# Weight sums of the first up-projection block by accumulating DMA, shorter row sums on GpSimd, earlier loads for the second block

## What is computed

```python
mix = jnp.einsum('btm,md->btd', jnp.concatenate([attn, c], axis=-1), w_out) + b_out
x = layer_norm(ALPHA * x + mix, ln1_g, ln1_b)
h = jnp.einsum('btd,df->btf', x, ffn_w_up)          # 2048 -> 2 x 5504
h, new_ffn = causal_dwconv(ffn_hist, h, ffn_conv_w, ffn_conv_b)   # 3 taps
hu, hg = jnp.split(h, 2, axis=-1)
f = jnp.einsum('btf,fd->btd', jax.nn.silu(hg) * hu, ffn_w_down)
x = layer_norm(ALPHA * x + f, ln2_g, ln2_b)
```

## Time and profile before

| | us |
|---|---|
| median of three runs | 2166.41 (2166.27 to 2168.33) |
| the profiled execution | 2166.84 |
| its span, first to last instruction | 2165.1 |
| TensorE busy (matmuls) | 2073.1, 96% of the span |
| VectorE busy | 1417.8, 65% |
| ScalarE busy | 910.3, 42% |
| GpSimd busy | 421.8, 19% |

### The profile page before, as it was taken

The page is one execution under the profiler, slowest core; times in us unless marked ns, Lnnn a source line. Parts: engine busy times, 40 slices in busy tenths (PEclk is TensorE's granted clock), DMA queues, the critical chain, the costliest instruction groups (busy, mean ns, idle before and its releaser), DMA issues.

```text
span 2165.1 us, 41651 instructions
## 1 busy us (share of the span) xinstructions
PE 2073.1 (96%) x16109; PEld 2045.3 (94%) x16117; DVE 1417.8 (65%) x1918; ACT 910.3 (42%) x1264; POOL 421.8 (19%) x543
## 2 busy tenths in 40 slices
PE   8999999799984999999999999999999999999995
PEld 8999999699984999999999999999999999999994
DVE  3788888677587877777877777777764222334324
ACT  4344444333464555554455555454443111222223
POOL 0113122020630221121212121212121000004222
PEclk9999999799996999999999999999999999999998
DMA  6322222023545666666767676767658222332222
GB/s 223 103 77 74 73 75 85 20 69 113 175 141 185 184 190 179 186 182 183 189 184 185 181 186 179 199 174 191 178 180 291 91 89 88 118 108 86 86 78 83
DMA packets 93211, 306.36 MB, mean 142 GB/s; under 512 B 11908, under 2 KB 12676, under 8 KB 93120
## 3 DMA queue, kind: packets, MB, share of 16 engines
q1 hardware_dynamic: 74976, 243.22, 34.2%
q0 software_dynamic: 16992, 59.87, 14.3%
q10 hardware_dynamic: 1152, 1.96, 0.3%
HBM read 281.05 MB, written 23.97 MB: 141 GB/s over the span
## 4 chain that ended last, share of the span: by engine, by line
PE 86%; DVE 7%; issue 3%; ACT 2%; DMA 2%; POOL 0%; SPq 0%; ACTq 0%; POOLq 0%; DVEq 0%
PE acc L857 41%; PE acc L920 22%; PE acc L576 15%; PE acc L770 3%; PE acc L672 1%; PE acc L661 1%; PE acc L652 1%; DMA x_raw<-xT 1%; PE acc L585 1%; DVE resid L2031 0%; ACT w_hi L965 0%; DVE w_lo L1679 0%; DVE tb L1647 0%; DMA raw_a<-w_down 0%; DVE comb L1813 0%
## 5 line engine op out<-in xcount | busy, mean ns | idle before, releaser
L857 PE MATMUL acc<-comb,w_hi 128*128 128x274 f32 x4816 | 929.4, 292 | 29.3 <-DVE comb L1813 18.4
L857 PEld LDWEIGHTS acc<-comb,w_hi 128*128 128x128 f32 x4816 | 766.6, 190 | 30.9 <-issue 11.8
L857 PE MATMUL acc<-comb,w_lo 128*128 128x274 f32 x2408 | 698.6, 290 | 0.0
L920 PE MATMUL acc<-acts,w_hi 128*128 128x272 f32 x2752 | 461.4, 290 | 5.8 <-DVE resid L1975 2.2
L857 PEld LDWEIGHTS acc<-comb,w_lo 128*128 128x128 f32 x2408 | 462.2, 192 | 0.0
L920 PEld LDWEIGHTS acc<-acts,w_hi 128*128 128x128 f32 x2752 | 391.7, 189 | 6.8 <-issue 3.5
L920 PE MATMUL acc<-acts,w_lo 128*128 128x272 f32 x1376 | 285.5, 289 | 0.0
L1209 ACT ACTIVATE w_hi<-sum 128x1024 fp32r<-128x1024 f32 x172 | 182.2, 1059 | 231.2 <-PE acc L857 120.9
L1761 DVE TENSOR_TENSOR w_lo<-sum,w_hi 128x1024 fp32r<-128x1024 f32 x172 | 210.6, 1225 | 88.6 <-ACT w_hi L1209 85.5
L1761 DVE TENSOR_TENSOR w_lo<-raw_a,w_hi 128x1024 fp32r<-128x1024 f32 x127 | 155.0, 1221 | 98.9 <-ACT w_hi L1209 98.9
L920 PEld LDWEIGHTS acc<-acts,w_lo 128*128 128x128 f32 x1376 | 217.1, 189 | 0.0
(11 more groups left out here) (247 smaller groups left out, 2795.1 us busy)
## 6 DMA issues: line engine op xcount, KB each, us to landing
raw_a<-w_up SPq DMA_DIRECT2D x129, 512.0 KB, 6.2
stage<-w_stream SPq DMA_DIRECT2D x90, 512.0 KB, 3.5
sum<-w_up SPq DMA_DIRECT2D x87, 512.0 KB, 3.5
sum<-w_up POOLq DMA_DIRECT2D x86, 512.0 KB, 7.5
sum<-w_down SPq DMA_DIRECT2D x45, 448.0 KB, 3.3
sum<-w_down SPq DMA_DIRECT2D x24, 512.0 KB, 3.5
act_spill<-prod_f SPq DMA_DIRECT2D x43, 272.0 KB, 6.3
act_raw<-act_spill POOLq DMA_DIRECT2D x43, 272.0 KB, 4.1
```

The lines of the kernel that those rows point to most:

```text
L857: mm = pe.matmul(bank(BANK_OF[j]), wt[:, k * P:(k + 1) * P], prod_comb(j, k, b), start=start and q == 0, stop=stop and q == 2, skip_group_ ...
L920: mm = pe.matmul(acc[:, a, h, 0:D_TOK // 2], wt[:, w * P:(w + 1) * P], x[:, h * (D_TOK // 2):(h + 1) * (D_TOK // 2)], start=start and q == ...
```

## The change

1. Block 0's `sum_2` is made in DRAM-to-SBUF transfers: SyncE loads quarter 2 into it ahead of pass 20's weight, GpSimd adds quarter 3 after row sum 20 and quarter 0 after row sum 25, and, once VectorE has split it for product 1, quarter 1. `make_s2(0)` and `make_s4(0)` leave VectorE; blocks from 1 on keep both. `raw_a11` and `raw_a12` aren't loaded for block 0, and the counts of their semaphores are one lower from then on.
2. GpSimd sums `SUMMED` = 12 of the second half's rows. TensorE takes rows 12 to 15 itself: 12 and 13 in the middle of pass 31, 14 and 15 behind it. There are four buffers of squares instead of two.
3. Block 1's loads: A11 behind `sum_3` of block 0, `sum_1` and `sum_3` between and behind the last row stores, A12 and A22 behind them; GpSimd issues their accumulations ahead of its wait for the last split.

The diff, cut to its core (the three new semaphores' declaration is left out):

```diff
 ORDER0 = (1, 3, 4, 5, 2, 6, 7)
+SUMMED = KT - 4
 ROWS_AT = (0, 1, 3, 4, 5, 7, 8, 10)
...
-        resid = at("resid", [P, 2 * KT + 2, TOK], F32, r1)
+        resid = at("resid", [P, 2 * KT + 4, TOK], F32, r1)
         sq1 = resid[:, 2 * KT:, :]
...
-            square = 2 * KT + m % 2
+            square = 2 * KT + m % 4
             return resid[:, m:square + 1:square - m, half_cols[h]]
...
-            for i in range(N_OUT - 4):
-                if i == 2:
-                    sp.wait_ge(ln_out, CT)
-                load_out(i)
-
             def quarter(f, q):
...
-                sp.wait_ge(s2_made, f + 1)
+                sp.wait_ge(s2_made, f)
                 sp.wait_ge(up_lo, nth(f, 0))
...
                 sp.wait_ge(up_lo, nth(f, 4))
-                sp.wait_ge(s4_made, f + 1)
+                sp.wait_ge(s4_made, f)
                 load_a12(f + 1)
-                if p is not None:
-                    spill(f - 1, p)
+                spill(f - 1, p)
                 sp.wait_ge(up_lo, nth(f, 5))
...
-            load_a11(0)
-            load_s1(0)
-            for i in range(N_OUT - 4, N_PASS):
+            for i in range(N_PASS):
+                if i == 2:
+                    sp.wait_ge(ln_out, CT)
+                if i == KT + 4:
+                    sp.wait_ge(attn_out, KT)
+                    sp.dma_start(sum_2[:, :], dram["w_up"][2]).then_inc(s2_loaded, 16)
+                    load_s1(0)
                 load_out(i)
...
+            load_a11(1)
             for k in range(4):
...
             load_a22(0)
-            for k in range(4, 8):
+            for k in range(4, 6):
                 spill_rows(k, x1_spilled)
+            sp.wait_ge(up_lo, nth(0, 2))
+            load_s1(1)
+            for k in range(6, 8):
+                spill_rows(k, x1_spilled)
+            sp.wait_ge(up_lo, nth(0, 3))
+            load_s3(1)
             sp.wait_ge(x1_spilled, 64)
             sp.wait_ge(t_made, 16)
-            load_a12(0)
-            up_loads(0, None)
+            load_a12(1)
+            sp.wait_ge(up_lo, nth(0, 5))
+            load_a22(1)
             with sp.Fori(0, (FT - 4) // 3) as i:
...
             last = N_PROD * (FT - 1)
-            sp.wait_ge(s2_made, FT)
+            sp.wait_ge(s2_made, FT - 1)
             sp.wait_ge(up_lo, last + 1)
...
                         row_stats_begin()
+                        row_last(SUMMED)
+                        row_last(SUMMED + 1)
                     w = slice(k * P, (k + 1) * P)
...
-                pe.wait_ge(row_summed, KT + POOLED)
+                pe.wait_ge(row_summed, KT + SUMMED)
                 row_term(2, ln_sq1[:, 0, second_half], True, False)
                 row_term(3, ln_sq1[:, 1, second_half], True, False)
-                row_last(POOLED)
...
                 pe.wait_ge(row_squared, KT + m + 1)
-                return row_term(3, sq1[:, m % 2, second_half], False, m == KT - 1)
+                return row_term(3, sq1[:, m % 4, second_half], False, m == KT - 1)
...
                     row_term(1, ln_sq1[:, 1, first_half], True, True).then_inc(row_stat, 1)
+            row_last(KT - 2)
             row_last(KT - 1).then_inc(row_stat, 1)
...
                 act.wait_ge(row_added, i + 1)
-                if i >= 2:
-                    act.wait_ge(row_summed, i - 1)
-                act.activation(sq1[:, m % 2, t], resid[:, m, t], ACT.Square).then_inc(row_squared, 1)
+                if i >= 4:
+                    act.wait_ge(row_summed, i - 3)
+                act.activation(sq1[:, m % 4, t], resid[:, m, t], ACT.Square).then_inc(row_squared, 1)
...
             def hi_a11(f, n):
-                act.wait_ge(a11_in, f * 16 + 16)
+                act.wait_ge(a11_in, f * 16)
                 up_hi_of(n, raw_a11)
...
             def hi_s2(f, n):
-                act.wait_ge(s2_made, f + 1)
+                if isinstance(f, int) and f == 0:
+                    act.wait_ge(s2_first, 32)
+                else:
+                    act.wait_ge(s2_made, f)
                 up_hi_of(n, sum_2)
...
             def hi_a12(f, n):
-                act.wait_ge(a12_in, f * 16 + 16)
+                act.wait_ge(a12_in, f * 16)
                 up_hi_of(n, raw_a12)
...
             def hi_s4(f, n):
-                act.wait_ge(s4_made, f + 1)
+                if isinstance(f, int) and f == 0:
+                    act.wait_ge(s4_first, 16)
+                else:
+                    act.wait_ge(s4_made, f)
                 up_hi_of(n, sum_2)
...
                 dve.wait_ge(s1_summed, f * 16 + 16)
-                dve.wait_ge(a11_in, f * 16 + 16)
-                if not (isinstance(f, int) and f == 0):
-                    dve.wait_ge(up_lo, f * N_PROD)
+                dve.wait_ge(a11_in, f * 16)
+                dve.wait_ge(up_lo, f * N_PROD)
                 dve.tensor_tensor(sum_2[:, :], sum_1[:, :], raw_a11[:, :], ALU.add).then_inc(s2_made, 1)
...
-                dve.wait_ge(a12_in, f * 16 + 16)
+                dve.wait_ge(a12_in, f * 16)
                 dve.wait_ge(up_lo, nth(f, 1))
...
             dve.wait_ge(row_added, 2 * KT)
-            make_s2(0)
             row_variance(1)
...
             low(0, 5, 0, raw_a22)
-            make_s4(0)
             for g in range(GROUPS):
...
             st.wait()
-            for i in range(KT + POOLED):
+            for i in range(KT + SUMMED):
                 row_sums(i)
-                if i == KT + 10:
+                if i == KT + 4:
+                    pool.wait_ge(s2_loaded, 16)
+                    pool.dma_start(sum_2[:, :], dram["w_up"][3], accum_op=ALU.add).then_inc(s2_first, 16)
+                if i == KT + 6:
                     pool.wait_ge(s1_in, 16)
                     pool.dma_start(sum_1[:, :], dram["w_up"][3], accum_op=ALU.add).then_inc(s1_summed, 16)
+                if i == KT + 9:
+                    pool.wait_ge(s2_first, 16)
+                    pool.dma_start(sum_2[:, :], dram["w_up"][0], accum_op=ALU.add).then_inc(s2_first, 16)
             pool.wait_ge(s3_in, 16)
...
-            def up_block(f, first=False, last=False):
-                if not first:
-                    save(f - 1, 0, c12_made)
+            def up_block(f):
+                save(f - 1, 0, c12_made)
                 history(f, 1)
-                if not last:
-                    sum_s1(f + 1)
+                sum_s1(f + 1)
                 history(f, 0)
-                if not last:
-                    sum_s3(f + 1)
+                sum_s3(f + 1)
                 save(f, 1, c22_made)
...
+            pool.wait_ge(up_lo, nth(0, 1))
+            pool.dma_start(sum_2[:, :], dram["w_up"][1], accum_op=ALU.add).then_inc(s4_first, 16)
+            sum_s1(1)
+            sum_s3(1)
             pool.wait_ge(x1_early, 64)
...
             pool.wait_ge(fst_loaded, 16)
-            up_block(0, first=True)
+            history(0, 1)
+            history(0, 0)
+            save(0, 1, c22_made)
             with pool.Fori(1, FT - 1) as f:
```

2 lines of the change are left out of this document (1 added, 1 removed).

## The result

The changed kernel takes 2148.14 us (median of four, 2147.75 to 2150.2) where the kernel before took 2166.34 beside it (2164.9 to 2168.33): ratio 0.9917, interval 0.99 to 0.9934. The direction was right and the size was not: 18.2 us instead of 14.9, and the time lies 1.2 us under the range. The profiled execution took 2148.49 us, its span is 2146.6, the mean granted clock 0.985.

The account below looks back on a forecast made before the run. It took TensorE's waits from 620 to 704 us as the bound, set by GpSimd, then VectorE's queue, then a transfer. 5.1 + 1.14 + 8.67 = 14.9 us gave 2151.5 us, own range 2149.3 to 2153.5 (8 in 10: to 2156.0).

Follow-up runs that it names:

- e10: Changed kernel with e3's added VectorE instruction and 6 unused ones matmuls in TensorE's wait for u_three; mark to first down product 964.3 us against 964.2, whole time not measured.
- e3: Changed kernel with one unused VectorE addition of 1.14 us where make_s4(0) stood; 2150.14 us, ratio 0.9913 to 0.994 to the kernel before.
- e9: Changed kernel with unused ones matmuls in TensorE's gaps of block 0 (15, 6, 3, and 3 in the wait for u_three); 2149.45 us, ratio 0.9902 to 0.9929.
- e8: Changed kernel with more unused ones matmuls in TensorE's gaps of block 0 (36, 12, 7, and 6 in the wait for u_three); 2160.04 us.

## What to carry to other kernels

Cost the edit from the rows around it, but then look through the rest of the trace for waits that end on a transfer with little to spare: such a wait can change by a microsecond or two with an edit elsewhere, and from one execution to the next (1.97 to 3.47 us in four traces of before), and the range should hold it. A fixed landmark ahead of the change, and one behind, turned runs that differ by 3 us into stretches that agree within 0.6, so a few traces settle what medians leave open. Low clock time behind a wait is worth something only if nothing waits again a product later (e10), and an instruction taken off one engine's queue is worth only the distance to the next engine that is late (e3).

## What the runs showed of the hardware

- The same 1.5 to 3.5 us of idle time on TensorE is followed by slow steps in some places and kernels and not in others: 2.27 us none (four traces), 3.40 after 5.6 and 6.0 us at full clock 15 steps that begin 0.5 to 0.9 us late, 3.41 after 4.6 us at full clock 23 steps at once, 2.09 and 2.77 none, 2.15 fourteen, and one wait of 2.17 us none in seventeen traces and 14 or 15 in three. Matmuls without use in the wait remove them (e9, e10).
- A ones matmul of 274 columns takes 0.46 us as two records at full clock (e8, e9) and 0.99 at 1.2 GHz (before), where one of a product takes 0.13 and 0.23.
- VectorE's two splits take 3.15 us beside two sums back to back and 3.83 with a DMA issue between the sums: the pause lets one split through and moves the second sum, and the other split with it.
- One 512 KB load moved ahead of 774 KB of writes on its queue took 4.3 us off the kernel before and nothing off the changed one.
